# Gate matrix of a PEER layer: one-hot matmuls replaced by accumulating indirect DMAs into zeroed DRAM

## The chip, the cores and the metric

The kernel runs on one NeuronCore of a Trainium2 chip. The metric is the device time of one execution in microseconds (us): three runs of the kernel before gave 2272.19, 2266.70 and 2264.40 us, median 2266.7. Five engines work beside each other, each on its own list of instructions, and wait for each other through semaphores: PE (matmuls), ACT, DVE and POOL (elementwise work), SP (issues DMAs). POOL and ACT issue DMAs too.

## The reference, cut to what matters

One layer of a streaming encoder over 320 tokens: 256 prompt tokens and 64 sample tokens. Attention and a state-space mixer come first; the change lies in the second half, the PEER feed-forward over 128 x 128 = 16384 single-neuron experts:

```
s = einsum('thcd,hcnd->thcn', q, peer_keys)          # 8 heads, 2 halves, 128 keys
sv, si = top_k(s, 16)                                # 16 best keys of each half
cand = sv[:, :, 0, :, None] + sv[:, :, 1, None, :]   # 256 candidates a head
fv, fp = top_k(cand, 16)                             # 16 experts a head and token
g = softmax(fv)                                      # their gates
out = sum over h, k of  g * gelu(x . u[expert]) * v[expert]
```

So each token has 8 x 16 = 128 picks, each with an expert number (i * 128 + j) and a gate. Two heads of one token may pick the same expert; their gates then add up.

## The kernel before, in words

All matmuls run on split operands: a 1 MB block of weights is loaded by SP into one of four ring slots (`ring`), ACT writes its high part (`high_piece`, line 534, four quarters of 128 x 512 a block), another engine subtracts to get the low part, and PE multiplies high by high, high by low and low by high. `w_parts` holds one block: a quarter is rewritten as soon as PE has used it (`w_used`).

The prompt tokens don't gather experts: the kernel computes all 16384 hidden values for all 256 tokens and multiplies them by a **gate matrix** G[expert, token] that is zero wherever a token did not pick an expert. The experts are cut into three sections of 48, 48 and 32 blocks (`SECS`; block i holds the 128 experts of key i). Section 0 is what the title's words call section 1. In a section, `hidden` runs over its blocks (PE, lines 1593 to 1595 in section 0, then ACT's Gelu, line 825), then `outputs` (lines 1989 to 1991) runs over them again with peer_v; ahead of each output block DVE multiplies the hidden block by its gates (`weighted`), ACT makes the high part (`hidden_high`) and DVE the low part (`hidden_low`). The 64 sample tokens gather their experts' rows by indirect DMAs on POOL (line 522), 64 from peer_u and 64 from peer_v, consumed by DVE.

What sets the order around the change, engine by engine:

- **PE**: the four column groups of the query projection w_pq (16 blocks, 320 columns a matmul), with the key scores of a group (`key_scores`) in the next group; then section 0's hidden blocks, with key_scores(3), the transposes of the sample rows and, from block 24 on, `spread_gates` between quarters.
- **DVE**: after the normalisation, `top16` for each of 4 groups of heads and 3 token tiles; `normed_low` (the low parts of the prompt's activations, which section 0 reads) among group 2; then `picks_of(0)`, `picks_of(1)`: candidates, the 16 best and their expert numbers for all 8 heads of a token tile; `gates_of` (softmax); then 32 rounds that write one-hot matrices for 8 tokens (line 936, 128 x 1024), which `spread_gates` multiplies on PE, 256 matmuls of 128 x 128; then `picks_of(2)` for the sample tokens. DVE makes no low parts in section 0's hidden blocks.
- **ACT**: the high parts; Gelu; `gates_out` (line 849) takes each product of `spread_gates` from PSUM, and every 16 tokens sends 1 MB to `g_tmp` in DRAM; `gates_in` reads the gates back in chunks of 8 blocks, 1 MB each, the first two after block 39.
- **POOL**: `low_parts` (line 505), a loop over the 16 w_pq blocks and section 0's 48 hidden blocks; after that it loads `acc` and the sample rows and issues the gathers.
- **SP**: the weight blocks in order; a block waits for the low parts of the block four earlier.

Of the kernel before, what the change touches and what calls it, by code (L numbers as in the profile page):

```python
# [42 lines left out]
GI = 8  # L43
GCH = PK // GI
GT = 16
TP = T_PROMPT
GTB = TP // GT
# [18 lines left out]
GATE_EXP, GATE_FIRST, GATE_LAST, SAMPLE_EXP, SAMPLE_IDS = 22, 25, 37, 43, 46  # L66


def gate_batches(block):

    blocks, total = GATE_LAST - GATE_FIRST + 1, TP // 4
    return [m for m in range(total) if GATE_FIRST + m * blocks // total == block]
# [14 lines left out]
def build(nc, io):  # L87
# [8 lines left out]
    with ctx:  # L96
# [113 lines left out]
        cand, cand2 = at(18432, PH, 256), at(16384, PH, 256)  # L210
        eq_k = at(18432, PH * TOPK, TOPK)
# [8 lines left out]
        gate, pick_i, pick_j = at(base + 2376, NT, 128), at(base + 2760, NT, 128), at(base + 3144, NT, 128)  # L220
# [12 lines left out]
        g_stage = [ex(12288 + GT * PK * i, GT * PK) for i in range(2)]  # L233
        oneB = [ex(20480 + 1024 * i, 1024).rearrange("p (t j) -> p t j", t=8) for i in range(2)]
        oneA = [ex(22528 + 1024 * i, 1024).rearrange("p (t j) -> p t j", t=8) for i in range(2)]
        gT, iT, jT = (ex(28104 + TP * i, TP) for i in range(3))
# [9 lines left out]
        B_DVE = b_block(0)  # L246


        def bank(b, n=COLS):
# [10 lines left out]
            keys qT sc_mm sc_out gmx gex picks pick_tr iota_ps eqa one gs_mm gs_out gw0 gw1 gm0 gm1  # L260
# [89 lines left out]

        @block.sync
        def _(sp):
# [75 lines left out]
            for s in range(SECTIONS):  # L428
                with sp.Fori(0, SECS[s] // SLOTS) as i:
                    turn("peer_u", SEC_AT[s], a_block(s), i)  # L430
                if s == 0:
                    turn("peer_v", 0, b_block(0), 0)
                with sp.Fori(0, SECS[s] // SLOTS - (s == 0)) as i:
                    turn("peer_v", SEC_AT[s] + SLOTS * (s == 0), b_block(s) + SLOTS * (s == 0), i)
# [12 lines left out]
        def _(pool):  # L447
            for dst, src in S5IN:
                pool.dma_start(dst, src).then_inc(S["s5in"], 16)
            pool.memset(ones1, 1.0).then_inc(S["ones"], 1)  # L450
            for j in range(4):
# [47 lines left out]
            def low_parts(first, end):  # L499

                with pool.Fori(0, (end - first) // SLOTS) as i:
                    for k in range(SLOTS):
                        for q in range(4):
                            pool.wait_ge(S["w_hi"], i * (4 * SLOTS) + (4 * (first + k) + q + 1))
                            pool.tensor_tensor(w_parts[:, q, 1, :], ring[:, k, 512 * q:512 * (q + 1)], w_parts[:, q, 0, :].bitcast(F32),  # L505
                                               ALU.subtract).then_inc(S["w_lo"], 1)
# [9 lines left out]
            pool.wait_ge(S["gs_mm"], TP // 4)  # L516
# [9 lines left out]
        def _(act):  # L526
# [281 lines left out]
            queries_out(0)  # L808
            for b in range(5, N_PQ):
                high(B_PQ + b)  # L810
                if b > 12:
                    normed_high(b - 13)
# [8 lines left out]
            def gelu(s, k):  # L821

                if s == 0:
                    act.wait_ge(S["w_used"], 4 * (a_block(s) + k + 1))
                    act.activation(H[:, k, :], bank(k % 2, TP), ACT.Gelu_apprx_tanh).then_inc(S["h_g"], 1)
# [16 lines left out]
            def gates_out(m):  # L842

                tb, part = divmod(m, GT // 4)
                if part == 0 and tb >= 2:
                    act.wait_ge(S[f"gw{tb % 2}"], 16 * (tb // 2))
                act.wait_ge(S["gs_mm"], m + 1)
                stage = g_stage[tb % 2].rearrange("p (i t) -> p i t", t=GT)[:, :, 4 * part:4 * part + 4]
                act.activation(stage, bank(2 + m % 3).rearrange("p (t i) -> p i t", t=4), ACT.Copy).then_inc(S["gs_out"], 1)
                if part == GT // 4 - 1:  # L850
                    act.wait_ge(S["gs_out"], m + 1)
                    act.dma_start(io["g_tmp"][:, :, tb, :].rearrange("c p x -> p c x"),
                                  g_stage[tb % 2].rearrange("p (c x) -> p c x", c=GCH)).then_inc(S[f"gw{tb % 2}"], 16)

            def gates_in(c):
# [3 lines left out]
                act.dma_start(gstream[c % 2], io["g_tmp"][c].rearrange("p b x -> p (b x)")).then_inc(S[f"gm{c % 2}"], 16)  # L859

            act.wait_ge(S["x_sv"], 16)
            for s in range(SECTIONS):
# [3 lines left out]
                for b in range(n):  # L866
                    if b == n - 1:
                        hidden_high(s, 0)
                    gates = gate_batches(b) if s == 0 else []
                    for q in range(4):  # L870
# [3 lines left out]
                        for j, m in enumerate(gates):  # L874
# [57 lines left out]
        def _(dve):  # L932
# [537 lines left out]
            for e in range(TP // 8):  # L1470
                eight = slice(8 * e, 8 * e + 8)
                jj, ii, gg = (spread(w[:, eight].unsqueeze(2), P, 8, PK) for w in (jT, iT, gT))
                if e >= 2:
                    dve.wait_ge(S["gs_mm"], 2 * (e - 1))
# [641 lines left out]
```

## Time and profile before

| | us |
|---|---|
| runs (three) | 2272.19, 2266.70, 2264.40; median 2266.7 |
| profiled execution, span from first to last instruction | 2270.2 |
| profiled execution, own time: of the three runs only one is as long as its span | 2272.19 (2.0 around the span) |
| w_pq stage, PE's last matmul of 320 columns starts | 738.25 |
| section 0: first hidden matmul, first output matmul | 738.40, 1099.8 |
| sections 1 and 2, first hidden matmul of section 1 | 1369.2 |
| PE, DVE, ACT, POOL busy | 2182.4, 1711.6, 1120.6, 591.4 |

The page lists the busy time of each engine, then the span in forty slices, the DMA queues, the chain of work that ended last and the costliest groups of instructions. A row of a group names the line, the engine, the operation, what it writes and reads, the count, the busy sum with the mean of one, and the idle time ahead of it with what ended it. In section 0's hidden stage four engines feed PE at once, so the stage is read from what PE, POOL and DVE each do between 738 and 1100 us, not from the shares of the whole span.

### The profile page before, as it was taken

The numbers are of one execution on the slowest core, as the hardware profiler recorded it, in microseconds if no ns is written. First come the engines' busy times: TensorE is split into PE (matmuls) and PEld (weight loads), VectorE is DVE, ScalarE is ACT, GpSimd is POOL, SyncE is SP. The second block draws the span as 40 slices with busy tenths as digits, with TensorE's granted clock in tenths as the row PEclk, the third lists the DMA queues.
The fourth block names the chain that finished last, engine by engine and source line by source line (L and its number), as shares of the span: only waits on it lengthen the run. The fifth ranks groups of instructions, "written<-read, shape, count | busy, mean of one in ns | idle before, by whom it ended". The sixth has DMA issues, their size and how long they took to land.

```text
span 2270.2 us, 34759 instructions
## 1 busy us (share of the span) xinstructions
PE 2182.4 (96%) x12720; PEld 1907.4 (84%) x12720; DVE 1711.6 (75%) x2968; ACT 1120.6 (49%) x2099; POOL 591.4 (26%) x445
## 2 busy tenths in 40 slices
PE   7899899899999989999999999999999999999998
PEld 7786687778899989999888888888888888888887
DVE  8957884665466981888388888877778898878866
ACT  4233445654544534554455554555555554555554
POOL 4002330000176898548311111111101111111100
PEclk9899999999999999999999999999999999999999
DMA  6542236223443445676888997888779988787964
GB/s 228 127 119 76 75 98 226 95 87 118 154 169 142 158 149 186 214 226 230 279 326 347 376 359 297 327 318 327 285 285 359 358 349 333 306 335 302 350 218 162
DMA packets 126534, 537.55 MB, mean 237 GB/s; under 512 B 27648, under 2 KB 61872, under 8 KB 65680
## 3 DMA queue, kind: packets, MB, share of 16 engines
q1 hardware_dynamic: 61888, 358.62, 44.2%
q0 software_dynamic: 19888, 139.85, 14.9%
q10 hardware_dynamic: 44640, 37.56, 5.4%
q8 instruction: 68, 1.11, 0.2%
q14 instruction: 50, 0.41, 0.1%
HBM read 507.02 MB, written 28.38 MB: 236 GB/s over the span
## 4 chain that ended last, share of the span: by engine, by line
PE 54%; issue 20%; POOL 12%; DVE 11%; ACT 2%; ACTq 0%; DMA 0%; POOLq 0%; DVEq 0%
POOL w_parts L505 12%; PE psum L1968 10%; PE psum L1989 10%; PE psum L1990 10%; PE psum L1991 10%; PE psum L1969 5%; DVE experts L936 5%; DVE w_parts L936 3%; PE psum L1617 1%; DVE experts L1526 1%; PE psum L1619 1%; PE psum L1618 1%; ACT w_parts L534 1%; DVE experts L1521 1%; PE psum L1600 1%
## 5 line engine op out<-in xcount | busy, mean ns | idle before, releaser
L534 ACT ACTIVATE w_parts<-ring 128x512 fp32r<-128x512 f32 x1296 | 807.6, 630 | 822.2 <-PE psum L1991 339.4
L936 DVE TENSOR_TENSOR w_parts<-ring,w_parts 128x512 fp32r<-128x512 f32 x1040 | 703.1, 693 | 389.1 <-ACT w_parts L534 383.7
L1968 PE MATMUL psum<-x_parts,w_parts 128*128 128x512 f32 x1280 | 453.0, 399 | 3.1 <-DVE w_parts L936 1.2
L1593 PE MATMUL psum<-x_parts,w_parts 128*128 128x256 f32 (+1 forms) x1344 | 412.0, 307 | 25.2 <-POOL w_parts L505 13.8
L505 POOL TENSOR_TENSOR w_parts<-ring,w_parts 128x512 fp32r<-128x512 f32 x256 | 361.3, 1423 | 196.8 <-ACT w_parts L534 191.2
L1989 PE MATMUL psum<-w_parts,h_parts 128*128 128x512 f32 x1024 | 398.9, 390 | 4.6 <-DVE h_parts L936 2.7
L1991 PE MATMUL psum<-w_parts,h_parts 128*128 128x512 f32 x1024 | 398.4, 389 | 0.0
L1990 PE MATMUL psum<-w_parts,h_parts 128*128 128x512 f32 x1024 | 398.4, 389 | 0.0
L1594 PE MATMUL psum<-x_parts,w_parts 128*128 128x256 f32 (+1 forms) x1344 | 397.4, 296 | 0.0
L1595 PE MATMUL psum<-x_parts,w_parts 128*128 128x256 f32 (+1 forms) x1344 | 397.2, 296 | 0.0
L1969 PE MATMUL psum<-x_parts,w_parts 128*128 128x256 f32 x1280 | 358.7, 280 | 0.0
L1968 PEld LDWEIGHTS psum<-x_parts,w_parts 128*128 128x128 f32 x1280 | 240.3, 188 | 66.3 <-DVE w_parts L936 7.3
L1593 PEld LDWEIGHTS psum<-x_parts,w_parts 128*128 128x128 f32 x1344 | 257.3, 191 | 34.3 <-POOL w_parts L505 17.0
L1594 PEld LDWEIGHTS psum<-x_parts,w_parts 128*128 128x128 f32 x1344 | 257.9, 192 | 0.7
L1595 PEld LDWEIGHTS psum<-x_parts,w_parts 128*128 128x128 f32 x1344 | 257.5, 192 | 0.0
L1969 PEld LDWEIGHTS psum<-x_parts,w_parts 128*128 128x128 f32 x1280 | 241.6, 189 | 0.0
L1989 PEld LDWEIGHTS psum<-w_parts,h_parts 128*128 128x128 f32 x1024 | 192.2, 188 | 46.2 <-DVE w_parts L936 3.1
L1991 PEld LDWEIGHTS psum<-w_parts,h_parts 128*128 128x128 f32 x1024 | 192.2, 188 | 39.8
L1990 PEld LDWEIGHTS psum<-w_parts,h_parts 128*128 128x128 f32 x1024 | 192.2, 188 | 39.7
L936 DVE TENSOR_TENSOR experts<-experts 128x256 f32<-128x256 f32 (+10 forms) x329 | 193.7, 599 | 7.2 <-ACT experts L665 2.9
L522 POOL DMA_INDIRECT experts<-in_peer_v,experts x64 | 76.4, 1194 | 459.4 <-DVE experts L1526 376.8
L522 POOL DMA_INDIRECT experts<-in_peer_u_rows,experts x64 | 74.0, 1156 | 423.4 <-DVE experts L1521 422.5
(237 smaller groups left out, 2549.1 us busy)
## 6 DMA issues: line engine op xcount, KB each, us to landing
ring<-in_peer_u SPq DMA_DIRECT2D x128, 1024.0 KB, 4.8
ring<-in_peer_v SPq DMA_DIRECT2D x128, 1024.0 KB, 5.1
ring<-in_w_in SPq DMA_DIRECT2D x32, 1024.0 KB, 4.9
ring<-in_w_out SPq DMA_DIRECT2D x16, 1024.0 KB, 4.8
ring<-in_w_pq SPq DMA_DIRECT2D x16, 1024.0 KB, 4.8
g_tmp<-experts ACTq DMA_DIRECT2D x16, 1024.0 KB, 5.9
experts<-g_tmp ACTq DMA_DIRECT2D x16, 1024.0 KB, 8.1
experts<-in_xT SPq DMA_DIRECT2D x8, 640.0 KB, 9.0
```

The costliest lines, as they stand in the source:

```text
L505: pool.tensor_tensor(w_parts[:, q, 1, :], ring[:, k, 512 * q:512 * (q + 1)], w_parts[:, q, 0, :].bitcast(F32), ALU.subtract).then_inc(S["w ...
L522: pool.indirect_dma_start(rows[b], None, table, bass.IndirectOffsetOnAxis(ap=ids[:, k:k + 1], axis=0)).then_inc(S[f"gr{b}"], 16)
L534: act.activation(w_parts[:, q, 0, :], ring[:, b % SLOTS, 512 * q:512 * (q + 1)], ACT.Copy).then_inc(S["w_hi"], 1)
L936: return dve.tensor_tensor(out, a, b, op)
L1593: pe.matmul(out, w_parts[:, q, 0, c], moving(0), start=start, stop=False)
L1594: pe.matmul(out, w_parts[:, q, 0, c], moving(1), start=False, stop=False)
L1595: return pe.matmul(out, w_parts[:, q, 1, c], moving(0), start=False, stop=stop)
L1968: pe.matmul(bank(b % 2), w_parts[:, q, 0, 128 * d:128 * d + 128], both_of(dc), start=dc == 0, stop=False)
L1969: ins = pe.matmul(bank(b % 2, TP), w_parts[:, q, 1, 128 * d:128 * d + 128], both_of(dc)[:, 0:TP], start=False, stop=dc == DC - 1)
L1989: pe.matmul(out, high, w_parts[:, q, 0, :], start=first, stop=False)
L1990: pe.matmul(out, high, w_parts[:, q, 1, :], start=False, stop=False)
L1991: ins = pe.matmul(out, low, w_parts[:, q, 0, :], start=False, stop=last)
```

## The change

- **Zeroed DRAM.** `g_tmp` becomes a flat array of 128 x 128 x 256 cells of 4 bytes (16.8 MB), cell (i, j, token). POOL clears 1024 words of SBUF (`zeros`) once, and SP sends them out in 16 DMAs of 1 MB, two behind each of the w_in blocks 5 to 12. DVE's `states_begin` and the first gate wait for all of them.
- **One-hot work removed.** The one-hot rounds on DVE, `spread_gates` on PE, `gates_out` and its 16 DMAs on ACT, and the transposes of the picks are gone.
- **Single gates sent.** POOL issues 256 indirect DMAs (`gates_sent`), one for each pick number and prompt tile: 128 single gates, one from each partition, are added to their cells. They go in batches of 16; a batch waits for its cell numbers (`idx`), its gates (`gp`) and, two batches back, the landing of the same tile's batch. Ten of them stand between the low parts of w_pq blocks 11 to 15, the other 246 behind these. Then POOL waits for all to land and loads the first two gate chunks itself.
- **Picks two heads at a time.** `pair_picks` does in five parts what `picks_of` did for eight heads; pairs 0 to 3 (groups 0 and 1) run before section 0, `normed_low` behind them; the rest is cut into 60 steps, one every 2.5 quarters of section 0's hidden blocks (`late_step`). ACT's exponentials of a pair (`exponentials_of`) follow w_pq blocks 8, 9, 12 and 13, later ones stand in section 0.
- **Low parts.** DVE, not POOL, makes the low parts of section 0's 48 hidden blocks (192 quarters). POOL keeps those of w_pq.
- **Gates read back** in pieces of 1 KB (256 tokens of one expert) where it was 8 KB.

The core of the diff:

```diff
+            sp.wait_ge(S["zero"], 1)
             for b in range(SLOTS, N_IN):
                 load("w_in", b, b)
+                if 5 <= b < 13:
+                    for c in (2 * (b - 5), 2 * (b - 5) + 1):
+                        sp.dma_start(io["g_tmp"].rearrange("(c r a x) o -> c r a (x o)", c=GCH, r=P, a=2)[c],
+                                     spread(zeros.unsqueeze(1), P, 2, 1024)).then_inc(S["g_zero"], 16)
...
-            low_parts(B_PQ, B_DVE)
+            def gates_sent(g):
+                u, j = divmod(g, TOPK)
+                c, head, n = u // 4, u // 2 % 2, u % 2
+                k = 2 * TOPK * c + TOPK * head + j
+                if g == 0:
+                    pool.wait_ge(S["g_zero"], 16 * GCH)
+                if j == 0:
+                    pool.wait_ge(S["idx"], 2 * c + n + 1)
+                    pool.wait_ge(S["gp"], 2 * c + n + 1)
+                    if u >= 2:
+                        pool.wait_ge(S[f"sg{n}"], 16 * TOPK * (u // 2))
+                pool.indirect_dma_start(io["g_tmp"], bass.IndirectOffsetOnAxis(ap=ix[:, n, k:k + 1], axis=0), gate[:, n, k:k + 1], None,
+                                        compute_op=ALU.add).then_inc(S[f"sg{n}"], 16)
+            for b in range(N_PQ):
+                for q in range(4):
+                    pq_low(b, q)
+                    if b >= 11 and q % 2:
+                        gates_sent(2 * (b - 11) + q // 2)
+            for g in range(10, 2 * PICKS):
+                gates_sent(g)
             pool.wait_ge(S["sid"], 64)
+            for n in range(2):
+                pool.wait_ge(S[f"sg{n}"], 16 * PICKS)
+            for c in range(2):
+                pool.dma_start(gstream[c].rearrange("p (i t) -> p i t", i=GI), gates_of_keys(c)).then_inc(S[f"gf{c}"], 16)
...
+            for c in range(2):
+                keys_top(c, 0, range(4))
+                if c:
+                    gates_done(1)
+                else:
+                    token_numbers()
+                for part in range(PAIR_PARTS):
+                    pair_picks(2 * c, part)
+                keys_top(c, 1, range(4))
+                for part in range(PAIR_PARTS):
+                    pair_picks(2 * c + 1, part)
+                gates_done(2 * c)
+                keys_top(c, 2, range(4))
+            keys_top(2, 0, range(4))
+            gates_done(3)
+            for i in range(4):
+                normed_low(i)
...
+            for quarter in range(4 * SECS[0]):
+                low(a_block(0) + quarter // 4, quarter % 4)
+                late_step(quarter)
             weighted(0, 0)
...
-                    for j, m in enumerate(gates):
-                        if 4 * j // len(gates) == q:
-                            spread_gates(m)
```

How the instructions move shows at three places. POOL, from the low parts of w_pq block 11 on: before, the loop body is one low part after another (the names: `w_parts` and `ring` are the weights, `experts` the large working buffer), and the gathers follow it:

```order
88 L505 TENSOR_TENSOR w_parts<-ring,w_parts 128x512 [waits w_hi]
89 L504 REGISTER_ALU
90 L505 TENSOR_TENSOR w_parts<-ring,w_parts 128x512 [waits w_hi]
91 L501 REGISTER_ALU
92 L501 COMPARE_AND_BRANCH
93 L512 DMA experts<-x_tmp 128x16x256 [waits x_sv,sid]
```

and now:

```order
59 L526 TENSOR_TENSOR w_parts<-ring,w_parts 128x512 [waits w_hi] x46
60 L541 DMA g_tmp<-experts 4194304x1 [waits gp,idx,g_zero]
61 L526 TENSOR_TENSOR w_parts<-ring,w_parts 128x512 [waits w_hi] x2
62 L541 DMA g_tmp<-experts 4194304x1
77 L526 TENSOR_TENSOR w_parts<-ring,w_parts 128x512 [waits w_hi] x2
78 L541 DMA g_tmp<-experts 4194304x1 x7
79 L541 DMA g_tmp<-experts 4194304x1 [waits gp,idx]
80 L541 DMA g_tmp<-experts 4194304x1 x15
81 L541 DMA g_tmp<-experts 4194304x1 [waits sg0,gp,idx]
```

The sends stand between the low parts of w_pq and then fill POOL's list, sixteen at a time, up to the gate loads.

DVE, at the start of section 0: before, the one-hot rounds fill the stage (three of their rows):

```order
887 L936 TENSOR_TENSOR psum<-psum,experts 128x1024 [waits one,gs_mm]
888 L936 TENSOR_TENSOR experts<-psum,experts 128x1024
889 L936 TENSOR_TENSOR experts<-psum,experts 128x1024 [waits eqa]
890 L936 TENSOR_TENSOR psum<-psum,experts 128x1024 [waits one,gs_mm]
891 L936 TENSOR_TENSOR experts<-psum,experts 128x1024
```

and now:

```order
837 L973 TENSOR_TENSOR experts<-experts 128x32
838 L973 TENSOR_TENSOR x_parts<-experts,x_parts 128x256 [waits x2_hi] x16
839 L973 TENSOR_TENSOR w_parts<-ring,w_parts 128x512 [waits w_hi]
840 L973 TENSOR_TENSOR experts<-experts 128x512
841 L973 TENSOR_TENSOR w_parts<-ring,w_parts 128x512 [waits w_hi,dve]
842 L973 TENSOR_TENSOR w_parts<-ring,w_parts 128x512 [waits w_hi]
843 L1435 MAX experts<-experts 128x8
844 L1438 MAX_INDEX experts<-experts 128x8 [waits dve]
845 L1439 MATCH_REPLACE experts<-experts 128x256
846 L1442 MAX experts<-experts 128x8 [waits dve]
847 L1445 MAX_INDEX experts<-experts 128x8 [waits dve]
```

Row 838, all 16 parts of `normed_low`, now stands behind the last gates of pair 3, and every low part of a weight quarter stands behind the pick steps ahead of it.

PE, a hidden block of section 0 between two quarters, before:

```order
4607 L1595 MATMUL psum<-x_parts,w_parts 128x256
4608 L1943 MATMUL psum<-experts 128x128 [waits one]
4609 L1943 MATMUL psum<-experts 128x128 x3
4610 L1943 MATMUL psum<-experts 128x128 [waits one]
4611 L1943 MATMUL psum<-experts 128x128 x3
4612 L1593 MATMUL psum<-x_parts,w_parts 128x256 [waits w_lo]
```

The rows of L1943 are gone, and a quarter's first matmul waits for DVE's count `v_lo` where it waited for POOL's `w_lo`.

## Rows read from the trace of the kernel before

**Rows 1.** The page: shares of the chain of work that ended last, by engine.

```profile
PE 54%; issue 20%; POOL 12%; DVE 11%; ACT 2%; ACTq 0%; DMA 0%; POOLq 0%; DVEq 0%
```

**Rows 2.** Stretch: section 0's hidden stage up to the one-hot rounds.

```profile
core 0: us, PE busy (x) PEld busy (x) DVE busy (x) ACT busy (x) POOL busy (x), PEclk, DMA share, GB/s
739.00:899.00 160.00, 150.30 (x1239) 148.39 (x1238) 106.14 (x295) 79.63 (x144) 146.78 (x100) 1.00 0.48 165
```

**Rows 3.** Groups by line from 739 to 1099 us.

```profile
L505 POOL TENSOR_TENSOR w_parts<-ring,w_parts 128x512 fp32r<-128x512 f32 x189 | 271.3, 1450 | 85.1 <-ACT w_parts L534 79.7
L1593 PE MATMUL psum<-x_parts,w_parts 128*128 128x256 f32 x767 | 222.9, 291 | 13.8 <-POOL w_parts L505 13.8
L1943 PE MATMUL psum<-experts 128*128 128x128 f32 x512 | 67.0, 278 | 3.5 <-DVE experts L936 3.5
```

**Rows 4.** PE's list in time (start, us): section 0 starts; 16 records of spread_gates.

```profile
738.40 0.28 PE L1593 MATMUL psum<-x_parts,w_parts 128*128 128x256 f32 x1
738.52 0.28 PE L1594 MATMUL psum<-x_parts,w_parts 128*128 128x256 f32 x1
...
936.69 1.95 PE L1943 MATMUL psum<-experts 128*128 128x128 f32 x16
938.39 0.36 PE L1593 MATMUL psum<-x_parts,w_parts 128*128 128x256 f32 x1
```

**Rows 5.** The output matmuls of line 1989: min/median/max ns, first to last start.

```profile
L1989 PE MATMUL psum<-w_parts,h_parts x1024: 387/389/498, 1099.8 to 2265.3; 128*128 128x512 f32 x171
```

**Rows 6.** POOL's list in time: a w_pq low part; two gathers that wait for nothing.

```profile
732.27 1.30 POOL L505 TENSOR_TENSOR w_parts<-ring,w_parts 128x512 fp32r<-128x512 f32 x1 [0.47 <-ACT w_parts L534]
...
1105.38 1.00 POOL L522 DMA_INDIRECT experts<-in_peer_u_rows,experts  x1 [0.30 <-issue]
1106.69 1.04 POOL L522 DMA_INDIRECT experts<-in_peer_u_rows,experts  x1 [0.30 <-issue]
```

**Rows 7.** POOL's lines 522 (gathers) and 505: min/median/max; the gathers' landing.

```profile
L522 POOL DMA_INDIRECT experts<-in_peer_u_rows,experts x64: 998/1155/1459, 1103.6 to 1599.5; - x64
DMA to landing us min/median/max: 6.8/7.8/30.4
...
L505 POOL TENSOR_TENSOR w_parts<-ring,w_parts x256: 1264/1295/3380, 606.1 to 1094.0; 128x512 fp32r<-128x512 f32 x128
```

**Rows 8.** DVE's list in time, 653 to 1100 us.

```profile
653.88 0.87 DVE L1397 MAX8 experts<-experts 128x8 f32<-128x128 f32 x4 [5.91 <-ACT experts L805]
659.32 0.87 DVE L1397 MAX8 experts<-experts 128x8 f32<-128x128 f32 x4
715.53 2.23 DVE L936 TENSOR_TENSOR x_parts<-experts,x_parts 128x256 fp32r<-128x256 f32 x4 [14.26 <-ACT x_parts L792]
766.12 2.29 DVE L936 TENSOR_TENSOR experts<-experts 128x2048 f32<-128x2048 f32 x1
805.21 3.43 DVE L936 TENSOR_TENSOR experts<-experts 128x2048 f32<-128x2048 f32 x1
890.67 0.29 DVE L936 TENSOR_TENSOR experts<-experts 128x128 f32<-128x128 f32 x1
1098.36 0.42 DVE L936 TENSOR_TENSOR experts<-experts 128x256 f32<-128x256 f32 x1
1099.63 1.29 DVE L936 TENSOR_TENSOR w_parts<-ring,w_parts 128x512 fp32r<-128x512 f32 x2
```

**Rows 9.** DMA issues, KB each and us to landing; q10's small packets, 320 to 345 us.

```profile
ring<-in_w_in SPq DMA_DIRECT2D x32, 1024.0 KB, 4.9
experts<-g_tmp ACTq DMA_DIRECT2D x16, 1024.0 KB, 8.1
y_tmp<-experts ACTq DMA_DIRECT2D x16, 80.0 KB, 3.3
...
q10 hardware_dynamic: 4224, 0.66, 17.8%
```

**Rows 10.** SP's waits for low parts in the front: us, times, longest.

```profile
SPq L358 <- DVE w_parts L936: 509.4, 48, 20.7
```

More of the change, by code:

```diff
@@ L63, with late_at, exp_at, gates_at @@
 B_EXP = B_PQ + N_PQ
[L66 to L72, printed above, removed]
+CELLS = PK * PK * TP
+PAIR_PARTS, KEY_PARTS = 5, 4
+PAIR_AT = {4: 0, 5: 9, 6: 22, 7: 31, 8: 40, 9: 45, 10: 50, 11: 55}
+KEYS_AT = {(2, 1): 5, (2, 2): 14, (3, 0): 18, (3, 1): 27, (3, 2): 36}
+LATE_STEPS = 60
+SAMPLE_EXP, SAMPLE_IDS = 39, 43
+def late_at(step):
+    return 5 * step // 2
+def exp_at(m):
+    return late_at(PAIR_AT[m] + 2) + 1
+def gates_at(m):
+    return exp_at(m) + 8
 def gather_at(section, product, k):
@@ L873, in _ @@
                             gelu(s, b - 1)
-                        for j, m in enumerate(gates):
-                            if 4 * j // len(gates) == q:
-                                gates_out(m)
+                        for m in range(4, 8):
+                            if s == 0 and exp_at(m) == 4 * b + q:
+                                exponentials_of(m)
                     if s:
@@ new lines, in gates_done, with sample_gates_done @@
+            def gates_done(m):
+                n, c = m % 2, m // 2
+                dve.wait_ge(S["gex"], m + 1)
+                g3 = gate[:, n, 2 * TOPK * c:2 * TOPK * (c + 1)].rearrange("p (h k) -> p h k", h=2)
+                chain(dve.tensor_reduce(gs[:, 0:2], g3, AX.X, ALU.add))
+                chain(dve.reciprocal(gs[:, 0:2], gs[:, 0:2]))
+                tt(g3, g3, spread(gs[:, 0:2].unsqueeze(2), P, 2, TOPK), ALU.mult).then_inc(S["gp"], 1)
+            def sample_gates_done():
+                r = T_SAMPLE
+                dve.wait_ge(S["gex"], 9)
+                g3 = gate[0:r, 2, :].rearrange("p (h k) -> p h k", h=PH)
@@ L1464, in _ @@
-            chain.wait()
-            dve.wait_ge(S["iota_ps"], 1)
-            dve.wait_ge(S["xs_sv"], 16)
-            all_keys = spread(psum[:, 7, 0:PK].unsqueeze(1), P, 8, PK)
-            eqA = psum[:, 5:7, :].rearrange("p b (t j) -> p (b t) j", t=4)
[L1470 to L1474, printed above, removed]
-                if e:
-                    dve.wait_ge(S["one"], 2 * e)
-                tt(eqA, all_keys, ii, ALU.is_equal).then_inc(S["eqa"], 1)
-                tt(oneB[e % 2], all_keys, jj, ALU.is_equal).then_inc(S["one"], 1)
-                dve.wait_ge(S["eqa"], e + 1)
-                tt(oneA[e % 2], eqA, gg, ALU.mult).then_inc(S["one"], 1)
@@ new lines, in _, with late_step @@
+            keys_top(2, 0, range(4))
+            gates_done(3)
+            for i in range(4):
+                normed_low(i)
+            def late_step(quarter):
+                for m, first in PAIR_AT.items():
+                    for part in range(PAIR_PARTS):
+                        if quarter == late_at(first + part):
+                            pair_picks(m, part)
+                for (c, n), first in KEYS_AT.items():
+                    for k in range(KEY_PARTS):
+                        if quarter == late_at(first + k):
+                            keys_top(c, n, (k,))
+                for m in range(4, 8):
+                    if quarter == gates_at(m):
+                        gates_done(m)
+                if quarter == late_at(LATE_STEPS):
+                    dve.tensor_copy(eid[0:T_SAMPLE, :], eid_f[0:T_SAMPLE, :]).then_inc(S["eid"], 1)
+                if quarter == 4 * SAMPLE_EXP + 8:
+                    sample_gates_done()
@@ L1934, in _, with hidden @@
             pe.wait_ge(S["sc_out"], 3 * NT)
[L1936 to L1947 removed]
+            def hidden(s, i, b, waits):
                 for q in range(4):
[L1950 to L1953 removed]
+                    pe.wait_ge(S["v_lo"], i * 16 + (4 * (a_block(s) + b - B_DVE) + q + 1))
                     for d in range(4):
```

213 lines of the change are left out of this document (89 added, 124 removed).

## The prediction

> **What bounds the kernel now.** I read the chain by engine first [rows 1]: POOL and DVE hold 12% and 11% of it, so the end is not PE's alone. Then the stage that the change rewrites, section 0's hidden blocks: from the first hidden matmul at 738.40 [rows 4] to the first output matmul at 1099.8 [rows 5], 361.4 us. The reader is to see there what PE itself needs. Its matmuls of 256 columns start 0.12 us apart [rows 4], so a quarter of twelve takes 1.44 us and the 192 quarters 276.5 us. The 512 records of spread_gates [rows 3] go at 1.70 us for 16 [rows 4], 54 us. That leaves 31 us: 13.8 waiting for POOL's low parts and 3.5 for the one-hot matrices [rows 3], and 13.6 of small work and edges, which the change leaves. POOL is nearly as full as PE: 146.8 of 160 us [rows 2]. The granted clock there is 1.00 [rows 2], the upper level of 2.4 GHz, and PE stays fed in the change, so I cost nothing for the clock.
>
> Behind the stage sections 1 and 2 keep their instructions, so what the change is worth is the shift of 1099.8. That matmul needs two things in the changed kernel: PE through its hidden blocks, and the first gates read back behind the last of POOL's sends. I work out both lines; the later one decides.
>
> **PE's line.** Its start moves. DVE now does, ahead of the low parts that section 0 needs: seven groups of top16 at 5.44 us (653.88 to 659.32, [rows 8]), 38.1; token numbers 0.8 (three operations near 0.29); four pairs; four gate sums of three operations near 0.29, 3.4; sixteen normed_low at 2.23 us for four [rows 8], 8.9. A pair: the picks of eight heads ran from 766.12 to 805.21 [rows 8], 39.1 us, a quarter of it 9.8. The operations outside the top16 don't shrink in number: 13 for a pair against a quarter of 10. The same operation takes 0.29 us on 128 elements and 2.29 on 2048 [rows 8], so about 0.16 us is fixed; 10.5 of these are 1.7, and a pair is 11.5 us, four 46. The sum: 653.9 + 38.1 + 0.8 + 46 + 3.4 + 8.9 = 751.1, and 0.7 for the first low part: PE starts at 751.8, not 738.4.
>
> From there PE needs 276.5 + 13.6; the spread and the waits for POOL and the one-hot matrices are gone. Are DVE's low parts in time? In the 150 quarters that carry steps PE takes 216 us. DVE has 150 low parts at 0.65 (1.29 for two, [rows 8]), 97.5; eight pairs, 92; five groups of top16, 27, and 3 for cutting them into single keys; four gate sums, 3.4: 223, so 7 us too much. The last 42 quarters are PE's again. PE's line: 751.8 + 276.5 + 13.6 + 7 = 1048.9, 51 us before 1099.8.
>
> **POOL's line.** The last low part of w_pq ends at 733.6 [rows 6]. Ten sends among the last twenty add 14.6 us at the price below against gaps of about 0.45 each, 9 in all, so 5.6 remain; and ACT's fourth exponential waits for pair 3's maximum: 653.9 + five groups (27.2) + 0.8 + three pairs (34.5) + two gate sums (1.7) + half a pair (5.5) = 723.6, some 4 us behind the place where ACT makes the next high part now. POOL is free for the other 246 sends at 743.
>
> The price of a send the trace doesn't show; the gathers are the nearest rows, 128 rows by 128 indices as well. Two that wait for nothing start 1.31 us apart, 1.00 busy and 0.30 between [rows 6]. The median gather, with DVE at work beside it, is 1.155 us [rows 7]; with the 0.30, 1.46. The low end is lower still: nothing excludes that 4 bytes need less than 8 KB, and below 1.19 PE's line ends last, so that is all a cheap send can bring. On the high end, a send reads its cell, adds and writes, and I take the longest gather of line 522 with 0.30 [rows 7] and round up to 1.9. I take 1.46: it is the row for an indirect DMA beside a busy DVE, which is what the sends will be.
>
> So: 743 + 246 x 1.46 = 1102.1; 3.3 until the last lands, as the shortest of scattered stores [rows 9]; 8.1 for the first gate chunk, as such a read lands now [rows 9]; 1.4 from the gate product at 1098.36 to the output matmul [rows 8, 5]. That is 1114.9, **15 us later** than 1099.8. By this line the stage that PE could finish 51 us earlier ends later than before: each 0.01 us in a send is 2.5 us at the end, and 1.40 is the point of no change.
>
> **What costs nothing.** Zeroing: 16 DMAs of 1 MB at 4.9 us or so [rows 9] go out in twos behind eight loads. SP waits 48 times there for DVE's low parts, 509 us in all [rows 10], 10.6 us a load; two of these DMAs are 9.8. Without that cover eight pairs would cost 78. DMA engines in the stage: the share is 0.48 [rows 2]; 4224 small packets took 17.8% of 16 engines for 25 us, 17 ns each [rows 9]; 32768 cells at that are 35 us of all engines, and four times that still fits in 300. Reading gates in 1 KB pieces: 14 later chunks, each with more than 30 us to land; at worst 1 us a chunk. ACT's five exponentials of pairs lie in its idle time. POOL's acc and row loads come 10 us before the output blocks, as far ahead as they need.
>
> **The sum.** The profiled execution took 2270.2 us of span and, if it is one of the three, 2272.2 in all; with 15 more 2287. The median of the runs is 5.5 lower: 2266.7 + 15 = **2282**. Under 0.3% (6.8 us) I call two times the same.
>
> Two rules against the change are weighed here. The gathers land 7.8 us after their issue but start 1.31 apart [rows 6, 7], so landing overlaps. The Trainium skill, DMA: Bandwidth & Descriptors, section "Anatomy of one DMA", gives a DMA issued from GpSimd some 2.0 us fixed, and its rules call transfers under 64 KB mostly overhead; as an estimate by that page, 246 sends one behind the other are 492 us and the end 148 us later. POOL's own subtraction takes 1.295 us in the median and up to 3.38 [rows 7] with DVE beside it. The Trainium skill, SBUF — State Buffer, section "Who interferes with whom", says that a DVE instruction with two SBUF inputs blocks a GpSimd one that reads SBUF, and that descriptor generation starves beside DVE's two-port modes; the low parts now on DVE have two SBUF inputs. No run shows a send beside them.
>
> **The rivals.**
>
> *A: cheap sends, faster.* If a send costs 1.31 as the unhindered gathers, POOL's line ends 246 x 0.15 = 37 us earlier: 22 us faster, 2245. For it: those are the two rows that start without a wait, and DVE is idle part of the time. Against it: they are two, and read whole rows without an addition. It decides between 1.19 and 1.37 us a send. Chance 0.24.
>
> *B: PE's line ends last, faster.* Under 1.19 us a send the hidden blocks decide: 51 us faster, 2216. For it: a send moves 512 bytes, a gather 1 MB. Against it: no indirect DMA here has started closer than 1.31 behind another. Chance 0.18.
>
> *C: dear sends, slower.* A batch of 16 may start only when the batch two before has landed, and each cell is read, added to and written; if descriptors, or DVE at the shared port, make a send 1.9 us, POOL ends 246 x 0.44 = 108 us later than in the forecast: 2390. Against it: the landing of a batch has the next batch's 23 us to hide in. It decides above 1.7 us. Chance 0.16.
>
> *D: the picks are late, slower.* DVE's small operations wait for POOL's low parts in w_pq: if a pair takes 16 us there (half a subtraction's wait for some seven operations), pairs 0 to 3 end 18 us later, ACT's fourth exponential holds the last two w_pq blocks, and POOL is free near 770 instead of 743; even at 1.31 a send the end is 5 us later than before, at 1.46 it is 42 (2309). Chance 0.04.
>
> *E: no change*, with sends of 1.37 to 1.43, where the gain and the new wait cancel. Chance 0.08.
>
> **How the numbers follow.** The forecast, sends of 1.43 to 1.7 that end the stage, has 0.30, the most of any case; its own range is 2273 to 2341. Faster is A and B, 0.42; same E, 0.08; slower the forecast, C and D, 0.50. The range leaves out about 1 in 10 on each side: it reaches down to PE's line, 2216, and up to C at 1.9, 2390.
>
> **What would show it.** The sends' line on POOL: 256 of them, the distance between two starts near 1.46, and the last near 1102; a gap on PE of some 60 us between the last hidden matmul (near 1049) and the first output matmul, put down to DVE's hidden_low, behind it the gate product and the DMA from g_tmp. Section 0's first hidden matmul near 752, its quarters 1.44 us where no step stands, a little over where pairs stand. No change in the front's 390 us and in sections 1 and 2. Wrong if the last send starts before 1080: then A or B; if POOL waits for its own landings (sg) between batches: C; if w_pq's last blocks wait for ACT by over 10 us: D.

## The result and the profile after

The changed kernel takes **2426.8 us** (median of four runs, 2418.3 to 2432.0; the kernel before 2267.9 beside it), a ratio of 1.070 with an interval of 1.068 to 1.072. It is slower by 159 us: the direction is the forecast's, the size is more than ten times its 15 us, and the time lies above the range.

Where the time is shows in the first place in a table by stage of the profiled execution (stretch in us, its length, then busy time and instructions of PE, of PE's weight loads, DVE, ACT and POOL, granted clock of TensorE as a share of 2.4 GHz, share of the DMA engines, GB/s):

```profile
940.00:1000.00 60.00, 58.71 (x484) 57.98 (x483) 57.70 (x133) 28.01 (x50) 50.24 (x30) 1.00 0.66 177
...
1050.00:1100.00 50.00, 11.88 (x100) 11.68 (x98) 3.88 (x6) 3.71 (x7) 41.78 (x28) 0.66 0.33 43
1100.00:1150.00 50.00, 0.00 (x0) 0.00 (x0) 0.00 (x0) 0.00 (x0) 41.78 (x28) 0.50 0.22 0
```

PE, DVE and ACT have nothing to do from about 1062 to 1250, and POOL goes on at 28 instructions in 50 us: the sends. The waits from 700 to 1290 us (who waited for whom: us in total, times, longest) name the same chain from its other end:

```profile
ACT h_parts L898 <- DVE experts L973: 192.4, 1, 192.4
DVE experts L973 <- DMA experts<-g_tmp: 191.5, 1, 191.5
...
PE psum L2044 <- DVE h_parts L973: 190.6, 1, 190.6
...
POOL g_tmp L541 <- issue: 77.2, 254, 1.2
...
ACT experts L859 <- DVE experts L973: 29.0, 2, 17.3
...
POOL w_parts L526 <- ACT w_parts L579: 20.3, 2, 13.6
```

One wait of 191 us, handed on from the gates' DMA through the gate product and the high and low parts to the first output matmul. POOL itself waits for no landing: its 77.2 us are 254 gaps of 0.30 between two sends, and no row has it waiting for a batch (sg). POOL's list in time, around the beginning and the end of the 246 sends that stand behind w_pq's low parts:

```profile
751.38 1.55 POOL L541 DMA_INDIRECT g_tmp<-experts  x1 [0.17 <-issue]
752.39 3.12 POOL L526 TENSOR_TENSOR w_parts<-ring,w_parts 128x512 fp32r<-128x512 f32 x2
...
761.83 1.56 POOL L541 DMA_INDIRECT g_tmp<-experts  x1 [0.30 <-issue]
...
1237.07 1.55 POOL L541 DMA_INDIRECT g_tmp<-experts  x1 [0.30 <-issue]
1238.93 1.55 POOL L541 DMA_INDIRECT g_tmp<-experts  x1 [0.30 <-issue]
1242.63 1.93 POOL L556 DMA_DIRECT2D experts<-g_tmp  x2 [2.15 <-DMA g_tmp<-experts]
```

A send that nothing disturbs is 1.55 busy and 0.30 to the next, **1.86 us**, where a gather that waits for nothing is 1.31 [rows 6]. Over all, from one start to the next: (1238.93 - 761.83) / 245 = **1.95 us**. A send that stands alone between two low parts takes 1.55 as well (751.38), so it is not a queue of earlier sends that makes it long. The groups by line of the two halves, 760 to 1000 and 1000 to 1270, part the price from the disturbance (busy, mean ns | idle before):

```profile
L541 POOL DMA_INDIRECT g_tmp<-experts x119 | 203.4, 1709 | 37.0 <-issue 37.0
...
L541 POOL DMA_INDIRECT g_tmp<-experts x129 | 203.1, 1574 | 39.3 <-issue 39.3
```

With DVE at work a send takes 1.71 in the mean and 0.30, nearly alone 1.57 and 0.30: DVE costs 0.14 us in the mean, the rest is the send's own. The 0.14 is not spread over all of them. Of the 246 sends 45 take more than 1.7 us, all of them before 1060, while DVE works; 188 stay under 1.6. The longest, and what DVE does beside it:

```profile
769.36 4.59 POOL L541 DMA_INDIRECT g_tmp<-experts  x1 [0.30 <-issue]
```

```profile
765.87 5.45 DVE L973 TENSOR_TENSOR x_parts<-experts,x_parts 128x256 fp32r<-128x256 f32 x16
...
772.55 1.29 DVE L973 TENSOR_TENSOR w_parts<-ring,w_parts 128x512 fp32r<-128x512 f32 x2
```

It begins in the middle of `normed_low` and ends at 773.95, 0.1 us behind the last of DVE's subtractions that follow without a gap (773.84). That it waits for them is read from the times; no run tried it.

PE's list in time shows where section 0 starts, where its hidden blocks end, and the first output matmuls:

```profile
772.02 0.55 PE L1665 MATMUL psum<-x_parts,w_parts 128*128 128x256 f32 x1 [9.12 <-DVE w_parts L973]
...
772.58 0.41 PE L1667 MATMUL psum<-x_parts,w_parts 128*128 128x256 f32 x1
772.80 0.41 PE L1665 MATMUL psum<-x_parts,w_parts 128*128 128x256 f32 x1
...
1061.60 0.28 PE L1667 MATMUL psum<-x_parts,w_parts 128*128 128x256 f32 x1
...
1252.51 0.77 PE L2044 MATMUL psum<-w_parts,h_parts 128*128 128x512 f32 x1 [190.63 <-DVE h_parts L973]
1253.08 0.63 PE L2045 MATMUL psum<-w_parts,h_parts 128*128 128x512 f32 x1
1253.50 0.63 PE L2046 MATMUL psum<-w_parts,h_parts 128*128 128x512 f32 x1
```

The first output matmul starts at 1252.51, before at 1099.8 [rows 5]: 152.7 us later. From there to the end it is 1175.3 us, before 2270.2 - 1099.8 = 1170.4: 4.9 more. Together 157.6, the difference of the two spans. Of the 4.9 the clock has some 2: PE has stood for 190 us, the granted clock is 0.50 (the lower level, 1.2 GHz), and some ten matmuls go 0.43 us apart before the distance falls to 0.23.

### The profile page after: what moved, and what is told of

The parts are those of the page before. It is cut to its first block, busy times and chain, and to the rows that moved or that the text cites. A ratio compares the mean times of both kernels' runs of the same rounds, so it can differ in the third digit from the quotient of the medians.

```text
span 2427.8 us, 33644 instructions
## 1 busy us (share of the span) xinstructions
PE 2132.4 (88%) x12202; PEld 1855.4 (76%) x12202; DVE 1755.5 (72%) x3213; ACT 1089.4 (45%) x2048; POOL 736.4 (30%) x512
## 4 chain that ended last, share of the span: by engine, by line
PE 58%; POOL 17%; DVE 15%; issue 5%; ACT 3%; DMA 1%; ACTq 0%; DVEq 0%; POOLq 0%
POOL g_tmp L541 17%; PE psum L2026 10%; PE psum L2044 9%; PE psum L2045 9%; PE psum L2046 9%; DVE experts L973 6%; PE psum L2027 5%; DVE w_parts L973 3%; PE psum L1665 2%; PE psum L1667 2%; PE psum L1666 2%; PE psum L1689 1%; ACT w_parts L579 1%; PE psum L1691 1%; PE psum L1690 1%
## 5 line engine op out<-in xcount | busy, mean ns | idle before, releaser
L973 DVE TENSOR_TENSOR w_parts<-ring,w_parts 128x512 fp32r<-128x512 f32 x1232 | 829.6, 693 | 413.3 <-ACT w_parts L579 405.8
L541 POOL DMA_INDIRECT g_tmp<-experts x256 | 419.3, 1638 | 78.8 <-issue 77.2
L973 DVE TENSOR_TENSOR experts<-experts 128x256 f32<-128x256 f32 (+11 forms) x371 | 196.8, 540 | 199.8 <-DMA experts<-g_tmp 191.5
```

The costliest lines, as they stand in the source:

```text
L541: pool.indirect_dma_start(io["g_tmp"], bass.IndirectOffsetOnAxis(ap=ix[:, n, k:k + 1], axis=0), gate[:, n, k:k + 1], None, compute_op=ALU. ...
L973: return dve.tensor_tensor(out, a, b, op)
```

## The experiments

Two theories were to be told apart. **P**: the end of the stage is POOL's line alone, and a send is dear in itself, on the engine (P1: through the addition; P2: as any scatter of single words). **L**: the sends are held back by their landings or by the DMA engines; beside it W, that VectorE or the reading of gates holds the stage as well.

### No sends, and half of them

```diff
-                    if b >= 11 and q % 2:
-                        gates_sent(2 * (b - 11) + q // 2)
-            for g in range(10, 2 * PICKS):
-                gates_sent(g)
+            pool.wait_ge(S["g_zero"], 16 * GCH)
```

> All 256 sends are left out (the prompt tokens' gates stay zero); zeroing, picks, low parts on VectorE and the reading of the gates stay. Theory P (POOL's line alone sets the end of section 0's hidden stage): the first output matmul follows the last hidden matmul, about 1062 in the changed kernel, by some 3 us, so about 187 us earlier than 1252.5: about 2238 us, 30 us under the kernel before. Rival W (VectorE with low parts and picks, or the reading of gates in 1 KB pieces, holds the stage as well): the first output matmul stays later than 1085 and the time is above 2260.

Measured: 2227.2 us, 0.982 (0.981 to 0.984) of the kernel before, 11 us under the expectation. PE's list of this run:

```profile
760.53 0.55 PE L1660 MATMUL psum<-x_parts,w_parts 128*128 128x256 f32 x1 [5.43 <-DVE w_parts L968]
...
1048.47 0.28 PE L1662 MATMUL psum<-x_parts,w_parts 128*128 128x256 f32 x1
1048.59 0.40 PE L2039 MATMUL psum<-w_parts,h_parts 128*128 128x512 f32 x1
```

The first output matmul follows the last hidden one at once, at 1048.6. So zeroing, low parts on DVE, picks by pairs and the later 1 KB reads hold nothing behind PE's line: W falls. (POOL issues the first two reads here at 1033.2, ahead of the end of PE's hidden blocks; in the changed kernel they stand behind the last send, and the first is 6.4 of the 13.6 us from that send to the output matmul.) Section 0 starts at 760.5 here; with sends, ten of them among w_pq's low parts, it starts at 772.0. That is most of the 13 us by which the expected 1062 was missed.

The second run leaves out every other send, 128 of 256, and halves the landings that are waited for:

```diff
-            for g in range(10, 2 * PICKS):
+            for g in range(20, 2 * PICKS, 2):
...
-                        pool.wait_ge(S[f"sg{n}"], 16 * TOPK * (u // 2))
+                        pool.wait_ge(S[f"sg{n}"], 8 * TOPK * (u // 2))
```

> Every second send is left out (half of the prompt tokens' picks have no gate), 128 instead of 256. Theory P: POOL sends 118 from about 760 at 1.95 us and is done near 990, before PE at 1062: the same time as without sends, about 2240 us, with PE and VectorE as much disturbed by the sends as in the changed kernel until 990. Rival W: later than the run without sends by over 10 us, since sends slow VectorE's low parts.

Measured: 2234.8 us, 0.986 (0.984 to 0.987). Line 541 of this run (min/median/max ns, first to last start), and below it the first output matmul of PE's list:

```profile
L541 POOL DMA_INDIRECT g_tmp<-experts x128: 1550/1557/4592, 699.6 to 998.1; - x128
```

```profile
1061.37 0.40 PE L2044 MATMUL psum<-w_parts,h_parts 128*128 128x512 f32 x1
```

The last send starts at 998, behind it PE still has 63 us of hidden blocks, and the kernel is 33 us faster than before. 128 sends are hidden, 256 are not: it is a matter of their number times their price. The run is 7.6 us over the one without sends, where P had no difference and W more than 10. Their first output matmuls lie 12.8 us apart, their first hidden matmuls 10.9 (771.4 and 760.5), so that while the sends run they cost PE about 2 us.

### What makes a send dear

```diff
-                pool.indirect_dma_start(io["g_tmp"], bass.IndirectOffsetOnAxis(ap=ix[:, n, k:k + 1], axis=0), gate[:, n, k:k + 1], None,
-                                        compute_op=ALU.add).then_inc(S[f"sg{n}"], 16)
+                pool.indirect_dma_start(io["g_tmp"], bass.IndirectOffsetOnAxis(ap=ix[:, n, k:k + 1], axis=0), gate[:, n, k:k + 1], None).then_inc(S[f"sg{n}"], 16)
```

> The sends write their cell instead of adding to it (where two heads pick the same key for a token, one gate is lost); number, cells and waits stay. Theory P1 (the addition is what a send costs more than a gather): a send takes 1.0 us and 0.30 as a gather that waits for nothing, the last starts near 1085 to 1110, about 2285 us. Theory P2 (POOL spends the time on any scatter of 128 single words): 1.56 and 0.30 as now, about 2427 us. Rival L (landing of the additions pushes back on the issue): the price falls, and falls less where the DMA engines carry weights.

Measured: 2298.8 us, 1.015 (1.012 to 1.017), 14 us over the expectation. Line 541 again, and below it the first of the 246 sends in POOL's list:

```profile
L541 POOL DMA_INDIRECT g_tmp<-experts x256: 963/972/2667, 700.2 to 1106.2; - x128
```

```profile
758.94 0.97 POOL L541 DMA_INDIRECT g_tmp<-experts  x1 [0.30 <-issue]
```

0.97 us instead of 1.56, with the same cells, the same number and the same waits: 0.58 us of each send is the addition. P1 holds, P2 falls. From one start to the next these sends take (1106.2 - 758.9) / 245 = 1.42 us over all, because beside DVE some are longer, where the expectation priced them at 1.30; the last one starts within its 1085 to 1110, but its time of 2285 was too short. And even so the kernel is 1.5% slower than before: from this start 256 indirect DMAs that only write don't fit behind PE either.

L falls too, by rows that are already shown. No row of the changed kernel has POOL waiting for a landing between its sends. The median adding send is 1.557 us in the run with half of the sends, all of them beside the loads of weights, and 1.55 from 1100 on, where the DMA engines are busy to 0.22 only. And a send that stands alone costs as much as one in a line.

The third run prices eight forms side by side, on the indices and gates of the same batches:

```diff
+                if u in (2, 3):
+                    pool.indirect_dma_start(io["g_tmp"], at_rows(P), gate[:, n, k:k + 1], None).then_inc(sent, 16)
+                elif u in (4, 5):
+                    pool.indirect_dma_start(io["g_tmp"], at_rows(64), gate[0:64, n, k:k + 1], None, compute_op=ALU.add).then_inc(sent, 16)
...
+                elif u in (8, 9):
+                    pool.indirect_dma_start(ex(word, 1), None, one, at_rows(P)).then_inc(sent, 16)
```

> The 16 batches of 16 sends are given other forms, each on its own line, to price them side by side (the prompt tokens' gates are wrong by it): adding 128 rows (7 batches and 3 sends), writing 128 rows, adding 64, adding 32, fetching single words by 128 rows, fetching 8 words by 128 rows, fetching single words by 64 rows, writing 64 rows. If POOL pays per index, 64 rows cost near half of 128's 1.56 us (0.8) and 32 a quarter (0.4) or a small fixed part more; if it pays per instruction, all stay near 1.5. P1: adding 1.56, writing and fetching near 1.0. P2: adding and writing 1.56, fetching 1.0. If single words are the cause, the fetch of one word costs 1.56 and that of eight less.

Measured: 2355.8 us (one run). 128 rows are added in 83 sends, that is five batches and three, where the expectation says seven. Lines, min/median/max ns; in this order writing 128 rows, adding 64, adding 32, fetching single words by 128 rows, fetching 8 words by 128, fetching single words by 64, writing 64, adding 128:

```profile
L549 POOL DMA_INDIRECT g_tmp<-experts x32: 965/1046/1494, 807.6 to 852.4; - x32
...
L551 POOL DMA_INDIRECT g_tmp<-experts x32: 1421/1474/1936, 854.1 to 912.7; - x32
...
L553 POOL DMA_INDIRECT g_tmp<-experts x32: 1324/1383/2307, 914.4 to 969.6; - x32
...
L555 POOL DMA_INDIRECT experts<-in_peer_v,experts x32: 945/1133/2684, 971.2 to 1018.7; - x32
...
L557 POOL DMA_INDIRECT experts<-in_peer_v,experts x13: 945/955/1412, 1020.0 to 1036.0; - x13
...
L559 POOL DMA_INDIRECT experts<-in_peer_v,experts x16: 893/898/961, 1074.0 to 1092.2; - x16
...
L561 POOL DMA_INDIRECT g_tmp<-experts x16: 892/897/932, 1093.4 to 1111.4; - x16
...
L563 POOL DMA_INDIRECT g_tmp<-experts x83: 1543/1552/4590, 701.0 to 1170.2; - x83
```

Compare the minima, which DVE has disturbed least. Direction and size hardly matter: writing 0.965, fetching one word 0.945, eight words 0.945. Rows matter little: 128 against 64 is 0.05 to 0.07 us, with addition 0.12, and 128 against 32 with addition 0.22. Drawn on to no rows at all, which no run has, an indirect DMA costs POOL some 0.83 us (0.893 less 64 rows at the 0.8 to 1.1 ns that a row costs), an adding one some 1.25 (1.324 less 32 rows at 2.3 ns); a row costs two to three times as much with an addition. So of the two prices in the expectation, by the index and by the instruction, the second holds for the most part, and single words are not the cause.

### The late start, and fewer additions

```diff
-                if b in (8, 9, 12, 13):
-                    exponentials_of((8, 9, 12, 13).index(b))
+                if b in (8, 9):
+                    exponentials_of(b - 8)
...
             queries_out(3)
+            for m in (2, 3):
+                exponentials_of(m)
```

> ACT's exponentials of pairs 2 and 3 move behind all of w_pq's high parts; nothing is left out. Theory S (the late picks hold ACT, ACT holds POOL's last low parts, and so the 246 sends start at 761.8 instead of some 743): the sends start 15 to 19 us earlier and the end comes as much earlier, about 2410 us; section 0's first hidden matmul stays near 772, since VectorE's own work decides that. Rival: the sends' start is set by POOL's own work (low parts slowed by VectorE, ten sends between them), not by ACT's waits: under 5 us gained, about 2424.

Measured: 2406.4 us, 1.062 (1.060 to 1.064) of the kernel before, 20.5 under the changed one. The first of the 246 sends in POOL's list, line 541, and the first hidden matmul of section 0 in PE's list:

```profile
736.29 1.56 POOL L541 DMA_INDIRECT g_tmp<-experts  x1 [0.30 <-issue]
```

```profile
L541 POOL DMA_INDIRECT g_tmp<-experts x256: 1549/1555/4584, 694.8 to 1212.9; - x128
```

```profile
771.11 0.55 PE L1667 MATMUL psum<-x_parts,w_parts 128*128 128x256 f32 x1 [34.52 <-DVE w_parts L975]
```

The 246 sends begin at 736.3 instead of 761.8 and end 26 us earlier, more than the 15 to 19 that were expected; section 0 starts on PE at 771.1, as expected hardly earlier, after 34.5 us of waiting for DVE's low part. S holds: ACT's waits for the pairs had cost the sends their start, and DVE sets PE's.

```diff
-                                        compute_op=ALU.add).then_inc(S[f"sg{n}"], 16)
+                                        compute_op=ALU.bypass if u < 2 else ALU.add).then_inc(S[f"sg{n}"], 16)
```

> As the run with late exponentials, and the sends of each token's first head (32 of 256) write their cell, which still holds its zero, instead of adding to it. Theory P1 (0.58 us for the addition in each send, all of it on the path): 32 x 0.58 = 18.6 us less than that run, about 2392. Rival: the price of a send is a queue's, not the instruction's, and 32 cheaper ones are made up for by the next: no difference, 2410.

Measured: 2389.6 us, 1.054 (1.053 to 1.056): 16.8 us under the last run, expected 18.6. To within 2 us the price is the instruction's own and is made up for nowhere. This is the best form of the changed kernel with all gates in place that I found, and it still loses 5.4%.

### A part of the change on the kernel before

Without sends the changed kernel is 41 us faster than the old one, so I asked whether the kernel before gains from low parts on DVE where its PE waits 13.8 us for POOL [rows 3].

```diff
+                    if q == 0 and b - a_block(0) in SHARED:
+                        pool.wait_ge(S["d_lo"], SHARED.index(b - a_block(0)) + 1)
+                        continue
...
+                if added[0] % SHARE_EVERY == 1:
...
+                        tt(w_parts[:, 0, 1, :], ring[:, block % SLOTS, 0:512], w_parts[:, 0, 0, :].bitcast(F32),
+                           ALU.subtract).then_inc(S["d_lo"], 1)
```

> The kernel before with one part of the change in small: VectorE makes the low part of the first quarter in 12 of section 0's blocks (6 to 17), between its operations of the picks; POOL makes the others; nothing is left out. Theory V (section 0 before loses some 10 of its 13.8 us of waits for POOL's low parts in this stretch, where VectorE's picks slow POOL): 8 to 12 us faster than before, about 2258. Rival: the picks come later by 12 low parts and waits for ACT's high parts, and the one-hot matrices behind them hold PE: no gain or a loss, 2268 or more.

Measured: 2269.8 us, 1.001 (1.000 to 1.002): no gain, V falls. The waits of 739 to 900 us, and below them two low parts of DVE's list in time:

```profile
POOL w_parts L520 <- DVE w_parts L949: 9.7, 3, 4.6
...
PE psum L1622 <- POOL w_parts L520: 7.4, 5, 1.6
...
PE psum L1622 <- DVE w_parts L949: 5.1, 2, 2.7
```

```profile
807.90 0.68 DVE L949 TENSOR_TENSOR w_parts<-ring,w_parts 128x512 fp32r<-128x512 f32 x1
818.26 0.67 DVE L949 TENSOR_TENSOR w_parts<-ring,w_parts 128x512 fp32r<-128x512 f32 x1
```

Between two of DVE's parts lie 10 us of picks, and POOL, then PE, wait for them. PE waits 7.4 us for POOL and 5.1 for DVE itself, 12.5 in all, where it waited 9.7 for POOL in the same stretch of the kernel before. The next run spaces the parts by time (its edit against the last run):

```diff
-SHARED, SHARE_EVERY = list(range(6, 18)), 8
+SHARED, SHARE_EVERY = list(range(6, 20)), 5.1
+PICK_US = [2.3] + [0.48] * 40 + [0.3] * 2 + [0.3, 2.3, 2.3, 2.3] * 2
...
-                if added[0] % SHARE_EVERY == 1:
+                if passed[0] >= passed[1]:
+                    passed[1] += SHARE_EVERY
```

> As the run before with shared low parts, but VectorE's share (first quarters of blocks 6 to 19) is placed by the time of its operations, one in 5.1 us of them, and not by their number. Theory V2 (in the last run the long operations left gaps of 10 and 13 us between two shared parts, in which POOL and PE waited for VectorE; evenly placed, most of the 13.8 us of waits go): 6 to 10 us faster than before, about 2259. Rival: whatever VectorE takes over it makes too late for PE as often as POOL did: within 3 us of 2267.

Measured: 2266.8 us, 0.999 (0.998 to 1.000). Its waits from 739 to 1100 us:

```profile
POOL w_parts L521 <- DVE w_parts L950: 16.5, 4, 5.4
...
PE psum L1626 <- POOL w_parts L521: 7.6, 6, 1.6
...
PE psum L1626 <- DVE w_parts L950: 4.6, 4, 1.7
```

PE's waits for POOL are down from 13.8 to 7.6 us, but 4.6 us of waits for DVE's own low parts have come in their place: 12.2 instead of 13.8. The first output matmul of the profiled execution starts at 1096.8 instead of 1099.8; in the median the gain is 1.5 us, not more than the measurement's uncertainty. V2 falls too: what DVE takes over is late for PE nearly as long as it was from POOL. No run with all of the gates in place beat the kernel before by more than that uncertainty.

## Why the prediction was wrong

The stage was read rightly: two lines, POOL's the later one, the output matmul behind the last send, and a gap on PE. The break-even of 1.40 us a send hung on the start at 743; from 761.8 it is 1.32 (1099.8 less 13.6 and 761.8, by 245). Term by term:

| step | forecast | measured |
|---|---|---|
| POOL free for the 246 sends | 743 | 761.8 |
| price of a send | 1.46 | 1.95 (undisturbed 1.86) |
| last send starts | 1100.7 | 1238.9 |
| from there to the first output matmul | 14.2 | 13.6 |
| first output matmul | 1114.9 | 1252.5 |
| PE starts section 0 | 751.8 | 772.0 |
| PE, start to the end of the hidden blocks | 297.1 | 289.7 |

**The step that failed is the price of a send**, "I take 1.46: it is the row for an indirect DMA beside a busy DVE". 0.49 x 246 = 120 of the 138 us; nearly all of the rest is the late start, 18.8. The row was of the right engine and number of rows, but of an instruction without addition: written instead of added, a send is indeed 0.97 and 0.30 undisturbed, like the gathers, and 1.42 over all, 0.04 under the forecast. The addition is 0.58 us of POOL's time, and the trace of before has no row with one. My high end (1.9, "a send reads its cell, adds and writes") holds the undisturbed 1.86 and just misses the 1.95; it was the longest gather rounded up, with no row for the addition. I chose by nearness of form and took the unknown part as nothing. A part that no row shows and that can only add should have moved the choice upwards.

**Rival C** had the price (1.9) and in part the reason. Its batch waits didn't occur: POOL has no wait for a landing in the changed kernel, and the last send has landed 3.1 us after its start (the forecast allowed 3.3 after its end). DVE's share is 0.14 us in the mean where it is busy, not the reason.

**Rival D happened as well**, at 0.04 the least likely of all. DVE's list in time shows two operations of the picks twice, beside POOL's low parts and while POOL waits for ACT:

```profile
664.63 1.68 DVE L973 TENSOR_TENSOR experts<-iota,experts 128x512 f32<-128x512 f32 x1
...
709.79 3.27 DVE L1456 CAST experts<-experts 128x64 f32<-128x64 uint32 x1
...
734.34 0.20 DVE L1456 CAST experts<-experts 128x64 f32<-128x64 uint32 x1
...
740.58 0.69 DVE L973 TENSOR_TENSOR experts<-iota,experts 128x512 f32<-128x512 f32 x1
```

1.68 against 0.69, 3.27 against 0.20. Pair 0 takes from 658.2 to 674.5, 16.3 us, pair 1 17.7, both before the first send at 700.2, and pair 3, in whose first nine us POOL stands still, 12.7; I had 11.5 for each. ACT's list shows what follows from it, the third and fourth exponential:

```profile
719.31 0.23 ACT L859 ACTIVATE experts<-experts 128x32 f32<-128x32 f32 x1 [11.62 <-DVE experts L973]
...
740.27 0.23 ACT L859 ACTIVATE experts<-experts 128x32 f32<-128x32 f32 x1 [17.35 <-DVE experts L973]
```

The fourth comes at 740.3, forecast 723.6, and the sends start 18.8 us late. That these two waits are the cause is shown by the run with late exponentials; that DVE is slowed by POOL's low parts is read from the durations and wasn't tried by a run. The range stopped at C because I held C and D for alternatives. C gave 2390 with D's 19 us left out; both together give 2409, and with D's own price, 27 us, 2417. That is still under the 2426.8: the send at 1.95 instead of C's 1.9 adds 12 us, and the part behind the first output matmul 4.9. 2390 + 18.8 + 12 + 4.9 is 2426.

**What held.** Zeroing costs nothing: the first top16 of w_pq's scores starts at 651.88, before at 653.88 [rows 8]. PE's line ends as forecast, but by luck: without sends the first output matmul is at 1048.6, and 1048.9 was the forecast, because a start 8.7 us later and a stage 9 us shorter cancel; with the sends the hidden blocks end at 1061.7. DMA engines are no bound: from 1100 to 1150 the sends alone hold 0.22 of the 16 engines, 0.22 x 50 x 16 / (28 x 128) = 49 ns for a cell, within the four times 17 that were allowed. Sections 1 and 2 are within 5 us of before. The clock was not quite free: "PE stays fed" is not so at the stage's two edges. Beside the 2 us above, it costs some 1.6 at 772, where PE comes from waits and 17 matmuls start 0.21 apart instead of 0.12; the granted clock there is 0.52, near the lower level:

```profile
772.00:776.00 4.00, 3.98 (x19) 4.00 (x20) 3.86 (x11) 0.63 (x1) 3.50 (x2) 0.52 0.10 0
```

Of the two rules set against the change the first came out nearly to the number, and by luck: 246 sends took 479 us, and the estimate by the Trainium skill, DMA: Bandwidth & Descriptors, "Anatomy of one DMA", was 492. The mechanism is another one, and without the addition the same sends take 1.42 instead of 1.95. That page of the Trainium skill puts most of the fixed time into the receipt of the write, and calls the making of descriptors small; here landings overlap (3.1 us to land, 1.86 from start to start), and it is POOL's own time for the instruction that adds up. On the second, the Trainium skill, SBUF — State Buffer, "Who interferes with whom", the trace agrees in direction, both ways round: a send beside DVE's subtractions takes 0.14 us more in the mean and 3.0 at most (4.59 for 1.55), and of the two pairs of rows above DVE's operations beside POOL's low parts take 1.0 us more (1.68 for 0.69) and 3.1 (3.27 for 0.20).

## What to carry to other kernels

An indirect DMA was paid here by the instruction, on the engine that issues it: 1.3 us from start to start, and 1.9 with an addition, only 0.22 less for a quarter of the rows. Multiply the price by the count and hold it against the stretch that is to hide it, before asking what the DMA engines can do. When a new operation is priced by its nearest row, name what the row lacks; if that part can only add, the estimate belongs above the row. And rivals that can both happen must be added up in the range.

## What the runs showed of the hardware

- An addition makes an indirect DMA 0.58 us longer on POOL (1.55 against 0.97 at 128 rows, 1.42 against 0.89 at 64); most of it doesn't fall with the rows. Why is open, since no run looks into the instruction.
- A gather of single words costs POOL what a gather of eight words by as many indices does (0.945 us), and what a scatter does (0.965).
- Behind an adding send two low parts of POOL take 3.1 us (row of 752.39 above), behind a writing send 2.56 in the run with the first heads written, 704 to 727 us. The row of the first low part begins 1.0 us after the send's start either way, so the send's last 0.5 us stand in both rows and count once: a send and two low parts are 4.3 us with the addition (751.38 to 755.68) and 3.7 without.
- Beside POOL's subtractions a small operation of DVE took 3.27 us instead of 0.20; beside DVE's subtractions a send of POOL took 4.59 instead of 1.55, in the mean 1.71. Both are read from the times alone.
